# Gathering the expert rows in another order, and the index copy behind the sixteenth dot

## The chip, the cores and the metric

The kernel runs on one core of one Trainium2 chip. The metric is the device time of the whole kernel in microseconds (us): 2663.45, the median of 3 runs (2663.09 to 2665.34).

## The reference

Two transformer blocks follow each other on 256 tokens of 2048 channels, all in float32. The change touches only the last stage of the second block, a retrieval of single-neuron experts ("PEER"), whose core is this:

```python
def chunk(zc):                                   # 128 tokens
    ...                                          # key scores, top 16 of each half, top 16 of the sums
    u = jnp.take(peer_u, expert, axis=0)         # expert: 128 tokens x 8 heads x 16
    act = jax.nn.gelu(jnp.einsum('chkd,cd->chk', u, zc))
    v = jnp.take(peer_v, expert, axis=0)
    w = (gate * act.astype(jnp.float32)).astype(zc.dtype)
    return jnp.einsum('chk,chkd->cd', w, v).astype(zc.dtype)
```

peer_u and peer_v have 16384 rows of 2048 floats (8 KB each). For every token and head 16 rows of either table are read.

## The kernel before

The first half of the kernel (up to about 1266 us) is dense matrix products, and the change doesn't touch it. The expert stage works in 16 **rows**, one for each half of the tokens (hf) and head; a row is 128 tokens, one for each partition, and 16 experts for each token, k = 0 to 15. Both halves run as a hardware loop over pairs of rows (par = 0, 1), so there are two loops of four turns on VectorE (DVE), ScalarE and TensorE (PE), and GpSimd (POOL) runs one loop of seven turns with the last two rows behind it.

For each row r and each k two **gathers** are made, indirect DMAs of 1 MB which fetch 8 KB for each of the 128 tokens: **U k** from peer_u into one of four buffers ubuf, **V k** from peer_v into one of four buffers vbuf (slot s = k % 4). GpSimd issues them all, in the order in which its program has them (`gather`, L590 to L596; in the trace the issue stands at L595). Each gather first waits until its slot is free.

What is done with them:

- VectorE waits for U k and makes a **dot** with the normed token (L1493), a product of two 128x2048 tiles with a sum into column k of act. The end of the dot frees the slot of ubuf (u_free).
- After the sixteenth dot it makes asq (L1497), ain (L1499), er (L1502), agx (L1504) and wk (L1508), with a tanh on ScalarE in between. wk holds the 16 weights of the row. Then comes `choose` (L1410), the **sort**: some 28 small dependent steps, which pick the experts of row r + 2 and leave their numbers in expf.
- ScalarE turns a weight k into a diagonal matrix (L972), and TensorE multiplies it with V k into four banks of PSUM, eight instructions of 128x512 (L1870). Their end frees the slot of vbuf (v_free). So V k of a row can be used only once the wk of its row is there, after all 16 dots of that row.

The U gathers run one row ahead of the V gathers: while V of row r is fetched, so is U of row r + 1. Here is the order of GpSimd in a row: V 0, V 1, V 2, then V 3, U 0, V 4, U 1 and so on up to V 15, U 12, and last U 13, U 14, U 15 of row r + 1 with no V between (LAG = 3, L604 to L611).

The row numbers for the gathers are in idx, two sets of columns taken in turn (par). The set which V of row r - 1 used is written anew for U of row r + 1 by the **index copy** (L1487), which stands ahead of dot 12. It waits until TensorE has used V 15 of row r - 1 (L1486), because that gather reads the old set. U 0 of row r + 1 waits for the copy (idx_ready, in `gather_u`, L598).

Of the kernel before, what the change touches and what calls it, by code (L numbers as in the profile page):

```python
# [36 lines left out]
PEER_HEADS, KEYS, TOPK = 8, 128, 16  # L37
# [104 lines left out]
def build(nc, T, out):  # L142
# [3 lines left out]
    with ctx:  # L146
        def sb(name, shape, dt=f32):
            return ctx.enter_context(nc.sbuf_tensor(name, shape, dt))

        S = {n: ctx.enter_context(nc.semaphore(n)) for n in ONCE + LOOPED}  # L150
# [4 lines left out]
        v_landed = [ctx.enter_context(nc.semaphore(f"v_landed{s}")) for s in range(4)]  # L155
        v_free = [ctx.enter_context(nc.semaphore(f"v_free{s}")) for s in range(4)]
# [17 lines left out]
        def view(region, at, *dims):  # L174
            n = int(np.prod(dims))
            v = region[:, at:at + n]
            if len(dims) == 1:
                return v
            names = "abcd"[:len(dims)]
            return v.rearrange(f"p ({' '.join(names)}) -> p {' '.join(names)}", **dict(zip(names, dims)))  # L180
# [63 lines left out]
        vbuf = [view(EX, (4 + s) * D, D) for s in range(4)]  # L244
# [47 lines left out]
        expf = sb("expf", [P, TOPK])  # L292
        idx = sb("idx", [P, 2, TOPK], u32)
# [39 lines left out]
        peer_u, peer_v = T["peer_u_2"][0], T["peer_v_2"][0]  # L333
# [117 lines left out]
        def _(g):  # L451
# [15 lines left out]
            for s in range(2):  # L467
                v = dup[:, s, :].rearrange("p (a n) -> p a n", a=2)
# [11 lines left out]
            for at, reps, n, step, base in parts:  # L480
                v = dist[:, at:at + reps * n].rearrange("p (a n) -> p a n", a=reps)
# [5 lines left out]
            for s, base in enumerate((CMP_LEN - 1, CMP_LEN - 1 - P)):  # L487
                v = cmask[:, s * NCP:(s + 1) * NCP]
# [101 lines left out]
            def gather(table, buf, landed, free, r, par, k):  # L590
                s = k % 4

                g.wait_ge(free[s], r * 4 + (k // 4 + 1))
                g.nop(nofuse=True)
                g.indirect_dma_start(buf[s], None, table,  # L595
                                     bass.IndirectOffsetOnAxis(ap=idx[:, par, k:k + 1], axis=0)).then_inc(landed[s], 16)  # L596

            def gather_u(r, par, k):  # L598
                if k == 0:

                    g.wait_ge(S["idx_ready"], r + 1)
                gather(peer_u, ubuf, u_landed, u_free, r, par, k)

            LAG = 3  # L604

            def gather_row(r, par, last=False):
                for k in range(TOPK + LAG):
                    if k < TOPK:
                        gather(peer_v, vbuf, v_landed, v_free, r, par, k)
                    if k >= LAG and not last:  # L610
                        gather_u(r + 1, 1 - par, k - LAG)  # L611

            for k in range(TOPK):
                if k in (0, 2):
# [5 lines left out]
            with g.Fori(0, ROWS // 2 - 1) as i:  # L620
                for par in range(2):
                    gather_row(i * 2 + par, par)
            gather_row(ROWS - 2, 0)
            gather_row(ROWS - 1, 1, last=True)


# [356 lines left out]
        def _(v):  # L983
# [470 lines left out]
            for j in range(8):  # L1454
# [12 lines left out]
                if j >= 1:  # L1467
                    v.wait_ge(S["sc_evac"], 1 if j < 5 else 2)
                    for part in {1: (0,), 2: (1,), 3: (2,), 4: (3,), 5: (4,), 6: (5, 6), 7: (7,)}[j]:
                        r = part // 4  # L1470
# [6 lines left out]
            for hf in range(HALVES):  # L1477
                with v.Fori(0, PEER_HEADS // 2) as i:
                    for par in range(2):
                        r = i * 2 + (PEER_HEADS * hf + par)  # L1480

                        for k in range(TOPK):
                            s = k % 4
                            if k == TOPK - 4:

                                v.wait_ge(v_free[3], r * 4 + 1)  # L1486
                                v.tensor_copy(idx[:, 1 - par, :], expf[:]).then_inc(S["idx_ready"], 1)  # L1487
                                v.wait_ge(S["idx_ready"], r + 2)
                            v.wait_ge(u_landed[s], r * 64 + 16 * (k // 4 + 1))
                            if k >= 2:  # L1490

                                v.wait_ge(u_free[(k - 2) % 4], r * 4 + ((k - 2) // 4 + 2))
                            v.tensor_tensor_reduce(out=junk[k % 2], in0=ubuf[s], in1=znat[:, hf, :], scale=1.0, scalar=0.0,  # L1493
                                                   op0=ALU.mult, op1=ALU.add, accum_out=act[:, par, k:k + 1]).then_inc(u_free[s], 1)
                        v.wait_ge(u_free[3], r * 4 + 5)

                        v.tensor_tensor(asq[:], act[:, par, :], act[:, par, :], ALU.mult).then_inc(S["gel_step"], 1)  # L1497
                        v.wait_ge(S["gel_step"], r * 3 + 1)
                        v.scalar_tensor_tensor(ain[:, par, :], asq[:], 1.0 / GELU_C, act[:, par, :], op0=ALU.add, op1=ALU.mult)\  # L1499
                            .then_inc(S["inner_ready"], 1)  # L1500
                        v.wait_ge(S["ex_done"], r + 1)
                        v.reciprocal(er[:, par:par + 1], es[:, par:par + 1]).then_inc(S["gel_step"], 1)  # L1502
                        v.wait_ge(S["gel_step"], r * 3 + 2)
                        v.scalar_tensor_tensor(agx[:, par, :], act[:, par, :], er[:, par:par + 1], eg[:, par, :], op0=ALU.mult, op1=ALU.mult)\  # L1504
                            .then_inc(S["gel_step"], 1)
                        v.wait_ge(S["gel_step"], r * 3 + 3)
                        v.wait_ge(S["gel_done"], r + 1)
                        v.scalar_tensor_tensor(wk[:, par, :], ath[:, par, :], 1.0, agx[:, par, :], op0=ALU.add, op1=ALU.mult)\  # L1508
                            .then_inc(S["w_ready"], 1)

                        v.wait_ge(S["sc_evac"], PEER_HEADS)
                        choose(r + 2, par, r * CHOOSE + 2 * CHOOSE)
# [384 lines left out]
```

## Time and profile before

| | |
|---|---|
| median of 3 runs | 2663.45 us |
| the profiled execution | 2671.37 us |
| its span, first to last instruction | 2669.6 us |
| busy: PE / DVE / POOL / ACT | 84% / 57% / 29% / 26% |
| L1870, products of the expert stage | 959.5 us, 2048 instructions |
| L1493, dots | 582.4 us, 256 instructions of 2291 ns |
| L595, gathers issued for V and U | 331.7 us and 295.9 us, 256 each |
| gathers, issue to landing | V 12.5 us, U 13.1 us (median) |
| moved by the gathers' queue | 539.07 MB in all |

The page cuts the span into 40 slices of 66.7 us; the expert stage is the last 20 of them. "Idle before" and the name behind the arrow in a row of the timeline tell how long the engine had nothing to do ahead of the instruction, and who released it. A row of the timeline begins with the start in us from the span's start and the duration in us.

### The profile page before, as it was taken

The page shows a single profiled execution, that of the slowest core. Times are in us where ns is not written, and L with a number is a line of the kernel's source. Part 1 is how long each engine was busy: PE and PEld are TensorE (multiplying, and loading weights), DVE is VectorE, ACT ScalarE, POOL GpSimd, SP SyncE. Part 2 cuts the span into 40 slices and gives each one's busy share as a digit, 9 for nine tenths or more (in the row PEclk, how much of TensorE's full clock was granted, in tenths as well). Part 3 has the DMA queues.
Part 4 walks back from the last instruction along what each step waited for, and adds up shares of the span by engine and source line. Part 5 has one row for each costly group of instructions (what it writes and reads, how often), then busy time and mean ns, then how long its engine had stood idle before and what let it go on. Part 6 is the DMA issues. An engine that isn't in the chain of part 4 may idle for free.

```text
span 2669.6 us, 33108 instructions
## 1 busy us (share of the span) xinstructions
PE 2230.4 (84%) x12212; PEld 1633.3 (61%) x12212; DVE 1528.6 (57%) x2181; ACT 694.6 (26%) x1151; POOL 772.3 (29%) x658
## 2 busy tenths in 40 slices
PE   7999999999999999899567668777687766877668
PEld 7999999999999999899522223222232322322223
DVE  4455555455646686656665555665556555566552
ACT  5344554444434435444100000000000000000001
POOL 3000000000002433120354444544445444444441
PEclk9999999999999999999788999998999889989899
DMA  9534444455675444565699999999999999999996
GB/s 260 184 127 142 141 143 140 157 163 169 213 228 177 142 158 158 154 193 158 234 394 396 400 423 393 400 402 390 416 401 400 389 386 423 402 387 403 388 423 248
DMA packets 280704, 754.61 MB, mean 283 GB/s; under 512 B 11968, under 2 KB 213152, under 8 KB 213792
## 3 DMA queue, kind: packets, MB, share of 16 engines
q0 software_dynamic: 74432, 539.07, 49.7%
q1 hardware_dynamic: 205936, 214.23, 25.3%
q8 instruction: 56, 0.92, 0.1%
q14 instruction: 40, 0.33, 0.0%
q10 hardware_dynamic: 240, 0.07, 0.0%
HBM read 751.22 MB, written 2.10 MB: 282 GB/s over the span
## 4 chain that ended last, share of the span: by engine, by line
PE 59%; DMA 25%; issue 7%; DVE 7%; POOL 1%; ACT 1%; DVEq 0%; POOLq 0%; ACTq 0%; SPq 0%
PE PS L1552 39%; DMA EX<-in_peer_v,idx 22%; PE PS L1870 14%; DVE EX L1493 2%; DMA RAW<-in_peer_u,idx 2%; PE PS L1687 1%; DVE WL L993 1%; POOL EX L595 1%; PE PS L1607 1%; PE PS L1665 1%; DVE XL L1003 0%; PE PS L1675 0%; PE PS L1787 0%; POOL RAW L595 0%; PE PS L1689 0%
## 5 line engine op out<-in xcount | busy, mean ns | idle before, releaser
L1870 PE MATMUL PS<-EX,RK 128*128 128x512 f32 x2048 | 959.5, 620 | 396.5 <-ACT RK L972 207.8
L1870 PEld LDWEIGHTS PS<-EX,RK 128*128 128x128 f32 x2048 | 390.9, 197 | 964.5 <-issue 902.2
L1552 PE MATMUL PS<-XH,WH 128*128 128x256 f32 x3024 | 839.1, 286 | 11.7 <-DVE WL L993 8.0
L1493 DVE CUSTOM_DVE_ANT_0 EX<-RAW,RZ 128x2048 f32<-128x2048 f32 x256 | 582.4, 2291 | 449.7 <-DMA RAW<-in_peer_u,idx 422.1
L1552 PE MATMUL PS<-XH,WL 128*128 128x256 f32 x3024 | 832.7, 284 | 0.0
L1552 PE MATMUL PS<-XL,WH 128*128 128x256 f32 x3024 | 761.9, 284 | 5.0 <-DVE XL L1003 3.1
L993 DVE TENSOR_TENSOR WL<-RAW,WH 128x1024 fp32r<-128x1024 f32 x380 | 479.7, 1274 | 413.5 <-ACT WH L643 410.9
L1552 PEld LDWEIGHTS PS<-XH,WH 128*128 128x128 f32 x3024 | 582.0, 192 | 15.7 <-issue 9.7
L1552 PEld LDWEIGHTS PS<-XH,WL 128*128 128x128 f32 x3024 | 582.2, 193 | 0.0
L643 ACT ACTIVATE WH<-RAW 128x1024 fp32r<-128x1024 f32 x380 | 400.2, 1059 | 566.1 <-PE PS L1552 564.5
L1552 PEld LDWEIGHTS PS<-XL,WH 128*128 128x128 f32 x3024 | 539.9, 193 | 5.9 <-DVE XL L1003 3.5
L595 POOL DMA_INDIRECT EX<-in_peer_v,idx x256 | 331.7, 1296 | 464.9 <-PE PS L1870 408.9
L595 POOL DMA_INDIRECT RAW<-in_peer_u,idx x256 | 295.9, 1156 | 362.4 <-DVE act L1493 211.8
L972 ACT ACTIVATE RK<-identh,wk 128x128 f32<-128x128 f32 x256 | 97.5, 399 | 759.7 <-PE PS L1870 752.8
L508 POOL TENSOR_SCALAR_AFFINE_SELECT RG<-RG 128x1024 f32<-128x1024 f32 x1 | 1.1, 1088 | 512.8 <-ACT RG L776 512.8
L966 ACT ACTIVATE ath<-ain 128x16 f32<-128x16 f32 x16 | 3.5, 216 | 483.1 <-DVE ain L1499 483.1
L514 POOL TENSOR_TENSOR RK<-RZ 128x512 f32 x16 | 17.1, 1067 | 215.5 <-DVE RZ L1259 148.8
L530 POOL MEMSET RK<- 128x1024 f32 x1 | 1.0, 954 | 181.3 <-PE PS L1759 181.3
L753 ACT ACTIVATE RG<-RG,nmx 128x256 f32<-128x256 f32 (+2 forms) x96 | 37.7, 394 | 45.7 <-DVE nmx L1146 45.7
L1487 DVE CAST idx<-expf 128x16 uint32<-128x16 f32 x16 | 3.0, 185 | 60.1 <-PE PS L1870 60.1
L567 POOL TENSOR_TENSOR RZ<-RZ 128x540 f32<-128x540 f32 (+3 forms) x10 | 15.1, 1507 | 55.3 <-DVE RZ L1291 54.8
L515 POOL TENSOR_TENSOR RK<-RK 128x512 f32<-128x512 f32 x16 | 26.9, 1681 | 1.3
(316 smaller groups left out, 1139.1 us busy)
## 6 DMA issues: line engine op xcount, KB each, us to landing
RAW<-in_w_in SPq DMA_DIRECT2D x110, 1024.0 KB, 5.1
RAW<-in_w_out SPq DMA_DIRECT2D x32, 1024.0 KB, 5.4
RAW<-in_w_ple_gate SPq DMA_DIRECT2D x16, 1024.0 KB, 5.4
RAW<-in_peer_wq SPq DMA_DIRECT2D x16, 1024.0 KB, 5.4
RAW<-in_w_up_a SPq DMA_DIRECT2D x8, 1024.0 KB, 5.4
RAW<-in_w_up_b SPq DMA_DIRECT2D x8, 1024.0 KB, 5.3
RAW<-in_peer_u,idx POOLq DMA_INDIRECT x256, 13.1
EX<-in_peer_v,idx POOLq DMA_INDIRECT x256, 12.5
```

The lines of the kernel that those rows point to most:

```text
L515: step(g.tensor_tensor(acc[:, 0], acc[:, 0], sqt[:, 0], ALU.add))
L595: g.indirect_dma_start(buf[s], None, table, bass.IndirectOffsetOnAxis(ap=idx[:, par, k:k + 1], axis=0)).then_inc(landed[s], 16)
L643: a.activation(WH[:, q], raw[:, slot, at:at + QUARTER_KT, :], ACT.Copy).then_inc(S["wh_ready"], 1)
L753: ins = a.activation(eT[:, at:at + size], sT[:, at:at + size], ACT.Exp, bias=nmx[:, n:n + 1], accum_out=sums[:, n:n + 1])
L972: a.activation(diag[:, s, :], identh[:], ACT.Copy, scale=wk[:, par, k:k + 1]).then_inc(diag_ready[s], 1)
L993: v.tensor_tensor(WL[:, q], raw[:, slot, at:at + QUARTER_KT, :], WH[:, q].bitcast(f32), ALU.subtract).then_inc(S["wl_ready"], 1)
L1493: v.tensor_tensor_reduce(out=junk[k % 2], in0=ubuf[s], in1=znat[:, hf, :], scale=1.0, scalar=0.0, op0=ALU.mult, op1=ALU.add, accum_out=act ...
L1552: ins = mm(o[:, t, :], w[:, q, k, c], x[:, n, :], start=(begins and k == t == m == 0), stop=(ends and k == QUARTER_KT - 1 and m == len(pai ...
L1607: ins = mm(bank(2 + s)[0:SPANS, 0:P], blocks, w1bd[:, s, l, :], start=(l == 0), stop=(l == CMP_LEN - 1))
L1665: mm(pS[:, 0:512], q1, kpad[:, par, :, bass.ds(i, 1), :].rearrange("p t g n -> p (t g) n"), start=True, stop=True)
L1687: mm(pO[:, at:at + size], vcur[:, n, cols], pts[:, src:src + size], start=(par == 0 and n == 0), stop=False, skip_group_check=True)
L1870: ins = mm(bank(4 * hf + c), diag[:, s, :], vbuf[s][:, 512 * c:512 * (c + 1)], start=False, stop=True, skip_group_check=True)
```

## The change

GpSimd's order becomes V 0, V 1, V 2, V 3, then U 0 to U 3 of the next row together, and from there V k, U k in turn up to V 15, U 15. The index copy, with its two waits, moves from ahead of dot 12 to behind ain, that is behind the sixteenth dot and ahead of er. No instruction is added or left out.

```diff
-            LAG = 3
+            HEAD = 4
 
             def gather_row(r, par, last=False):
-                for k in range(TOPK + LAG):
-                    if k < TOPK:
-                        gather(peer_v, vbuf, v_landed, v_free, r, par, k)
-                    if k >= LAG and not last:
-                        gather_u(r + 1, 1 - par, k - LAG)
+                for k in range(TOPK):
+                    gather(peer_v, vbuf, v_landed, v_free, r, par, k)
+                    if k >= HEAD - 1 and not last:
+                        for ahead in range(HEAD) if k == HEAD - 1 else (k,):
+                            gather_u(r + 1, 1 - par, ahead)
...
                         for k in range(TOPK):
                             s = k % 4
-                            if k == TOPK - 4:
-
-                                v.wait_ge(v_free[3], r * 4 + 1)
-                                v.tensor_copy(idx[:, 1 - par, :], expf[:]).then_inc(S["idx_ready"], 1)
-                                v.wait_ge(S["idx_ready"], r + 2)
                             v.wait_ge(u_landed[s], r * 64 + 16 * (k // 4 + 1))
...
                         v.scalar_tensor_tensor(ain[:, par, :], asq[:], 1.0 / GELU_C, act[:, par, :], op0=ALU.add, op1=ALU.mult)\
                             .then_inc(S["inner_ready"], 1)
+                        v.wait_ge(v_free[3], r * 4 + 1)
+                        v.tensor_copy(idx[:, 1 - par, :], expf[:]).then_inc(S["idx_ready"], 1)
+                        v.wait_ge(S["idx_ready"], r + 2)
                         v.wait_ge(S["ex_done"], r + 1)
```

## Rows read from the trace of the kernel before

**Rows 1.** The page: GB/s moved in 40 slices, and the chain's shares by engine.

```profile
GB/s 260 184 127 142 141 143 140 157 163 169 213 228 177 142 158 158 154 193 158 234 394 396 400 423 393 400 402 390 416 401 400 389 386 423 402 387 403 388 423 248
...
PE 59%; DMA 25%; issue 7%; DVE 7%; POOL 1%; ACT 1%; DVEq 0%; POOLq 0%; ACTq 0%; SPq 0%
```

**Rows 2.** Windows (us, busy of each engine, PEclk, DMA share, GB/s) of a row's turn.

```profile
1930.00:1938.00 8.00, 5.61 (x7) 2.52 (x8) 6.52 (x28) 1.49 (x5) 0.00 (x0) 0.50 1.02 424
1938.00:1942.00 4.00, 4.00 (x10) 1.72 (x10) 3.06 (x13) 0.40 (x1) 1.87 (x2) 0.99 0.30 88
```

**Rows 3.** Timeline of GpSimd at the same turn: U 13, V 2, U 0, V 4.

```profile
1908.23 0.93 POOL L595 DMA_INDIRECT RAW<-in_peer_u,idx  x1 [3.71 <-DVE act L1493]
...
1921.91 3.03 POOL L595 DMA_INDIRECT EX<-in_peer_v,idx  x1 [0.30 <-issue]
...
1927.46 1.91 POOL L595 DMA_INDIRECT RAW<-in_peer_u,idx  x1 [0.30 <-issue]
1939.73 0.94 POOL L595 DMA_INDIRECT EX<-in_peer_v,idx  x1 [10.36 <-PE PS L1870]
```

**Rows 4.** Timeline of VectorE at it: dot 15, asq, dots 0 and 1 of the next row.

```profile
1928.48 2.29 DVE L1493 CUSTOM_DVE_ANT_0 EX<-RAW,RZ 128x2048 f32<-128x2048 f32 x1
...
1930.81 0.17 DVE L1497 TENSOR_TENSOR asq<-act 128x16 f32<-128x16 f32 x1
...
1944.88 2.29 DVE L1493 CUSTOM_DVE_ANT_0 EX<-RAW,RZ 128x2048 f32<-128x2048 f32 x1 [0.50 <-DVE expf L1450]
...
1948.01 2.29 DVE L1493 CUSTOM_DVE_ANT_0 EX<-RAW,RZ 128x2048 f32<-128x2048 f32 x1 [0.83 <-DMA RAW<-in_peer_u,idx]
```

**Rows 5.** Timeline of TensorE: V 15, the next row's V 0 on, V 11 and V 15.

```profile
1917.70 3.67 PE L1870 MATMUL PS<-EX,RK 128*128 128x512 f32 x8 [1.30 <-DMA EX<-in_peer_v,idx]
1932.39 27.10 PE L1870 MATMUL PS<-EX,RK 128*128 128x512 f32 x56 [11.02 <-ACT RK L972]
...
1980.95 3.67 PE L1870 MATMUL PS<-EX,RK 128*128 128x512 f32 x8 [1.14 <-DMA EX<-in_peer_v,idx]
...
2000.82 3.67 PE L1870 MATMUL PS<-EX,RK 128*128 128x512 f32 x8 [1.29 <-DMA EX<-in_peer_v,idx]
```

**Rows 6.** The page's group of the index copy: busy, mean ns, idle before it.

```profile
L1487 DVE CAST idx<-expf 128x16 uint32<-128x16 f32 x16 | 3.0, 185 | 60.1 <-PE PS L1870 60.1
```

**Rows 7.** Waits from 1345.30 to 2601.83: us in total, times, longest us.

```profile
DVE EX L1493 <- issue: 19.4, 3, 6.7
...
DVE EX L1493 <- DVE idx L1487: 3.5, 15, 0.2
```

**Rows 8.** asq in all rows: number, min/median/max ns, first and last start.

```profile
L1497 DVE TENSOR_TENSOR asq<-act x16: 174/174/175, 1345.3 to 2601.8; 128x16 f32<-128x16 f32 x16
```

**Rows 9.** Timeline of VectorE: asq of rows 1, 9, 10, 12, 13, 14.

```profile
1429.40 0.17 DVE L1497 TENSOR_TENSOR asq<-act 128x16 f32<-128x16 f32 x1
...
2097.86 0.17 DVE L1497 TENSOR_TENSOR asq<-act 128x16 f32<-128x16 f32 x1
...
2183.21 0.17 DVE L1497 TENSOR_TENSOR asq<-act 128x16 f32<-128x16 f32 x1
...
2351.49 0.17 DVE L1497 TENSOR_TENSOR asq<-act 128x16 f32<-128x16 f32 x1
...
2434.46 0.17 DVE L1497 TENSOR_TENSOR asq<-act 128x16 f32<-128x16 f32 x1
...
2518.78 0.17 DVE L1497 TENSOR_TENSOR asq<-act 128x16 f32<-128x16 f32 x1
```

**Rows 10.** Timeline behind asq of row 9: dot 0 and the issue of U 4.

```profile
2118.07 2.29 DVE L1493 CUSTOM_DVE_ANT_0 EX<-RAW,RZ 128x2048 f32<-128x2048 f32 x1 [6.54 <-issue]
...
2121.14 2.24 POOL L595 DMA_INDIRECT RAW<-in_peer_u,idx  x1 [3.09 <-DVE act L1493]
```

**Rows 11.** DMA from 2097.86 to 2117.86, an instruction queue: packets, MB, share.

```profile
q14 instruction: 2, 0.02, 0.3%
```

**Rows 12.** Timeline of TensorE: the 16 V of the last row.

```profile
2603.41 57.00 PE L1870 MATMUL PS<-EX,RK 128*128 128x512 f32 x128 [11.01 <-ACT RK L972]
```

## The prediction

> **What bounds the kernel now.** I read the page's slices and chain first. In the last 20 slices the core moves 384 to 423 GB/s, where the dense half moves 127 to 260 for the most part [rows 1]. TensorE's 59% of the chain and the DMAs' 25% say little by themselves, since in the expert stage each V lands, is used, and frees a slot [rows 1]. So the question is whether the transfers ever run dry. In the middle of a row they don't: V 11 and V 15 are used 19.87 us apart, which is four pairs of gathers, 2.484 us a gather and 4.97 a pair [rows 5], and 424 GB/s is the rate of a full queue [rows 2]. A row has 32 gathers, so no row can take less than 32 x 2.484 = 79.5 us. An undisturbed one takes 2434.46 - 2351.49 = 82.97 us from asq to asq [rows 9]. The 3.5 us between are seen in the windows: 88 GB/s from 1938 to 1942, a loss of 4 x (1 - 88/424) = 3.2 us [rows 2].
>
> Next, the timeline tells why. Behind U 0 (issued at 1927.46) GpSimd issues nothing until V 4 at 1939.73, because V 4 needs the slot of V 0 [rows 3]. V 0 can't be used before wk, and TensorE starts it 1.58 us behind asq, after 11.02 us without work [rows 4, 5]. At the granted clock of 0.50 (the 1.2 GHz level; the window in which TensorE starts after that idle time) V 0 needs until 1938.95, if I take the 0.78 us that GpSimd takes to follow the end of a dot (2118.07 + 2.29 to 2121.14) for the end of a V too [rows 2, 3, 10]. That is 6.56 us in place of the 3.67 of other V [rows 5]. The gathers issued until then run out at about 1938. asq in turn is late, since the copy waits for V 15 (60.1 us in all 16 rows) and the last four dots come behind it [rows 6].
>
> **The new order at a row's turn.** I count from the use of V 15 of row r - 1 as time 0. The queue then lands U 15 at 2.48, V 0 to V 3 of row r at 4.97 to 12.4, U 0 to U 3 of row r + 1 at 14.9 to 22.4, and V 4 at 24.8. A gather that finds the queue empty needs, from the end of its issue until it can be used, 4.86 us: V 4's issue ends at 1940.67 and the dot on U 1, the second gather behind the gap, starts at 1948.01, 7.34 less 2.48 [rows 3, 4]. Now each against its turn:
> - V 3 has its slot at 3.67 + 0.78, its issue takes 0.94 [rows 3, 5], so it could be used at 10.3, ahead of 12.4. V 0 to V 2 have their slots before. Hidden.
> - U 15 arrives with nothing before it in the dots' way: asq is at 2.48 + 2.33 = 4.8 [rows 4]. The copy's wait for V 15 is over at 3.67, so the wait that cost up to 4 us per row ends. The copy costs 0.185 us plus 0.2 for the wait on its own semaphore, 0.4 in all, and it is now ahead of wk and of the sort [rows 6, 7]. What stands behind this wait on VectorE is er, agx, wk, the sort and the next dots; on GpSimd, U 0 and all gathers after it.
> - U 0 is released at 5.4 and usable at 11.2 (its turn: 14.9). U 1 to U 3 follow 1.24 us apart. V 4 needs V 0's end: TensorE starts at 4.8 + 1.58 + 0.4 = 6.8 after only 3.1 us of idle time, V 4 would be usable at 17, or at 20 if V 0 takes 6.56, and its turn is 24.8. So the gap of before closes.
> - **U 4** is late next. It needs dot 0, and dot 0 stands behind the sort: 1944.88 - 1930.81 = 14.07 us after asq, plus 0.4 for the copy [rows 4]. From the start of dot 0 to the end of U 4's issue there is one row that shows just this, dots back to back: 2118.07 to 2121.14 + 2.24 = 2123.38, 5.31 us [rows 10]. So U 4 is usable at 4.8 + 14.5 + 5.3 + 4.9 = 29.4, and its turn is 27.3. V 5 and all others stand behind it. A gap of 2.1 us replaces that of 3.5.
>
> After that, issues among back-to-back dots end once per dot, 2.2 us apart, and the queue takes 2.48, so it doesn't run dry again. From U 4 to U 15 are 22 turns, 54.65 us, and the new row takes 14.5 + 5.3 + 4.9 + 54.65 + 2.33 = **81.6 us**, 1.35 less than 82.97.
>
> The 2.24 us of U 4's issue against 0.94 elsewhere are part of this price. An issue that begins while a dot runs ends 0.88 us behind that dot's end: V 2, issued at 1921.91 during a dot, took 3.03 [rows 3, 10]. The Trainium skill, SBUF — State Buffer, "Who interferes with whom", says that VectorE and GpSimd share a port pair that the first to start holds for its whole instruction, and that a VectorE instruction with two SBUF inputs holds up those of GpSimd that read SBUF. The trace agrees: 3.03 against 0.94. Without such a hold, U 4's issue would end 1.3 us sooner, and the 14 full turns would gain 18 us more.
>
> **Where VectorE pauses.** Dot 0 is behind its row's asq by 14.07 us, but by 20.21 after asq of row 9 (2097.86 to 2118.07), and the idle time before it is put down to nothing but issue [rows 9, 10]. There are 3 such waits, 19.4 us [rows 7], all where the second half's loop turns back, and meanwhile an instruction queue moves packets [rows 11]. Now this is on slack: its rows take 85.35 and 84.32 us (rows 9 and 13), the third lies between, 1.9 over a row without it [rows 9]. In the new order U 4 waits for dot 0, so the pause of 6.1 is paid in full: 81.6 + 6.1 = 87.7, which is 2.9 us slower than now, or 4.8 if the 1.9 are something else that stays. I take the middle, 3.8 each. The loop bodies keep their instructions, so I expect the pauses to stay. The Trainium skill, Runtime: NRT & Kernel Launch, "Instruction fetch mechanics", says that a taken branch to a target outside the fetched window must first fetch it by DMA. The trace agrees with the place and the queue.
>
> **The sum** (us):
> - first turn: now 1429.40 - 1345.3 = 84.1, then 81.6: -2.5 [rows 8, 9];
> - 11 turns without pause: 11 x -1.35 = -14.9;
> - 3 turns with pause: 3 x 3.8 = +11.4;
> - the last row: its 57.00 us on TensorE have no U beside them and are bound by TensorE [rows 12]. 3.1 us of idle time instead of 11 leaves V 0 at 3.67, -2.9 (0 if the clock falls all the same); the copy +0.4. Together -2.5.
>
> That is -8.5. The profiled execution took 2671.37 with a span of 2669.6, 7.9 over the median (0.3%); I carry the difference over to the median: 2663.45 - 8.5 = **2655.0**. From the bounds: pauses at 2.9 or 4.8 give -11.2 or -5.5; a cold V 0 at the end gives -5.6; 0.3 us more or less per turn for an unqueued gather gives 4.5 either way. The likeliest case's own range is 2648 to 2662.
>
> **The rivals.** About 0.2% (5.3 us) is what can be told from no change.
> - *The pauses go* (10%). If the moved steps shift where the loop's code falls, these three turns also gain 1.35 each, and the 3 x 1.9 that they cost now if these are the pause's: -2.5 - 14 x 1.35 - 2.5 = -23.9, and -29.6 with them: 2634 to 2639.5. For it: the first half's three turns with the same body have no such pause [rows 7]. Against: the count of instructions doesn't change.
> - *The hold is less* (5%): U 4's issue isn't held up, -8.5 - 14 x 1.3: 2637. Against it are 3.03 and 2.24.
> - *The gap only moves* (13%). If U 4 is usable 0.5 us later than I count, 15 turns cost 7.5: 2662.5, no difference. For it: the price of an unqueued gather rests on one place.
> - *Slower* (12%): the sort pays. In the new order five issues (U 0 to U 3, V 4) fall into wk and the first half of the sort, where now there is none before 1939.73 [rows 3]. If the shared port makes one step of VectorE wait for one issue of 0.94 us in each of 15 turns, that is +14.1, and 2669. It decides from 8.5 / 15 = 0.57 us per turn on. Against it: the issue at 1939.73 falls into the sort now, and the 14.07 us already contain it.
> - The likeliest case has 60%: of these 42 over 0.2% faster, 17 within, 1 slower.
>
> Faster: 42 + 10 + 5 = 57%. Within 0.2%: 17 + 11 of the third rival = 28%. Slower: 12 + 2 + 1 = 15%. The range of 2636 to 2669 leaves out part of the first two rivals and half of the slower one.
>
> **What the profile would show.** Right: V 4 is no longer released by TensorE after 10 us of idle time; U 4 has the long wait on a dot instead, and its issue takes over 2 us. The copy has no idle time before it. Rows of 81.6 us and three of 87.7. TensorE sits idle for about 3 us before V 0, with the clock at 2.4 GHz. The low window in GB/s is about 2 us long and follows V 4. Wrong: a wait before V 3 or U 0 in which the rate falls; asq to dot 0 over 14.8 us; a second low window behind U 4; rows 9, 11, 13 no longer than their neighbours.

## The result

The changed kernel takes 2676.27 us (median of 6 runs, 2674.31 to 2681.12), where the kernel before takes 2663.22. The ratio is 1.0054, 95% interval 1.0041 to 1.0067: slower by half a per cent, some 13 to 14 us, where 8.5 us less were forecast. In the next section it is measured once more, at 2681.89 us and 1.0073 (1.0048 to 1.0099). The span of the profiled execution is 2673.5 us.

The rates and the chain of the page after. Beside [rows 1], TensorE has 8 points less of the chain and VectorE 4 more, and the slices of the expert stage are as full as before.

```profile
GB/s 261 183 126 133 149 144 141 149 166 173 208 222 183 137 167 158 154 193 158 237 397 399 398 415 402 404 400 403 421 404 405 360 407 418 363 403 361 423 400 264
...
PE 51%; DMA 26%; DVE 11%; issue 8%; POOL 3%; ACT 1%; DVEq 0%; POOLq 0%; SPq 0%; ACTq 0%
```

A row's turn in the timeline of GpSimd after (the order is V 4, U 4, V 5, U 5), to be read beside [rows 3]:

```profile
2016.02 0.93 POOL L595 DMA_INDIRECT EX<-in_peer_v,idx  x1 [0.37 <-issue]
2026.83 2.25 POOL L595 DMA_INDIRECT RAW<-in_peer_u,idx  x1 [9.88 <-DVE act L1488]
2029.38 1.90 POOL L595 DMA_INDIRECT EX<-in_peer_v,idx  x1 [0.30 <-issue]
2031.59 1.90 POOL L595 DMA_INDIRECT RAW<-in_peer_u,idx  x1 [0.30 <-issue]
```

V 4 no longer waits for TensorE (0.37 instead of 10.36 us). The long wait is now U 4's, for the end of dot 0, and three issues in a row take about 2 us each. The same turn on VectorE, with asq, the index copy, and dots 0, 4, 5 and 6 (beside [rows 4]; the dot stands at L1488 now):

```profile
2009.64 0.17 DVE L1492 TENSOR_TENSOR asq<-act 128x16 f32<-128x16 f32 x1
...
2009.94 0.17 DVE L1497 CAST idx<-expf 128x16 uint32<-128x16 f32 x1
...
2023.76 2.29 DVE L1488 CUSTOM_DVE_ANT_0 EX<-RAW,RZ 128x2048 f32<-128x2048 f32 x1 [0.22 <-DVE expf L1450]
...
2034.15 2.29 DVE L1488 CUSTOM_DVE_ANT_0 EX<-RAW,RZ 128x2048 f32<-128x2048 f32 x1 [1.46 <-DMA RAW<-in_peer_u,idx]
...
2040.95 2.29 DVE L1488 CUSTOM_DVE_ANT_0 EX<-RAW,RZ 128x2048 f32<-128x2048 f32 x1 [4.50 <-DMA RAW<-in_peer_u,idx]
...
2046.02 2.33 DVE L1488 CUSTOM_DVE_ANT_0 EX<-RAW,RZ 128x2048 f32<-128x2048 f32 x1 [2.77 <-DMA RAW<-in_peer_u,idx]
```

The copy no longer waits. Dot 0 is 14.12 us behind asq, dot 4 10.39 behind dot 0. Then comes what the prediction had named as a sign of being wrong, a second slow stretch behind U 4: from dot 4 to dot 5 are 6.80 us, where a pair of gathers takes 4.97. The windows of the turn show it too (us, busy of each engine, PEclk, DMA share, GB/s), beside [rows 2]:

```profile
2016.00:2024.00 8.00, 8.00 (x20) 3.55 (x19) 6.10 (x22) 0.80 (x2) 0.93 (x1) 1.00 1.02 425
2024.00:2030.00 6.00, 1.55 (x4) 0.38 (x2) 6.00 (x5) 0.40 (x1) 2.87 (x2) 1.00 0.85 318
2030.00:2034.00 4.00, 3.71 (x5) 1.50 (x6) 2.70 (x4) 0.00 (x0) 3.39 (x3) 0.62 0.87 334
2034.00:2036.00 2.00, 1.69 (x4) 0.52 (x2) 1.85 (x1) 0.27 (x1) 1.70 (x2) 0.91 1.02 389
2036.00:2038.00 2.00, 0.00 (x0) 0.00 (x0) 0.45 (x2) 0.13 (x1) 1.70 (x2) 0.95 1.00 373
2038.00:2040.00 2.00, 1.41 (x2) 0.84 (x3) 0.00 (x0) 0.00 (x0) 1.43 (x2) 0.50 1.00 410
```

The deep hole of before (88 GB/s for 4 us) is gone. In its place the rate is below 425 for 16 us. Against 425 that is a loss of 1.5 + 0.9 + 0.2 + 0.2 + 0.1 = 2.9 us (each window's length times one minus its rate over 425). It was 3.2 before.

Behind rows 9, 11 and 13 VectorE pauses as it did (3 waits put down to issue, 17.7 us in all). Here is dot 0 behind row 9, whose asq is at 2092.93, and the asq of row 10, 88.57 later [rows 9, 10]:

```profile
2112.87 2.29 DVE L1488 CUSTOM_DVE_ANT_0 EX<-RAW,RZ 128x2048 f32<-128x2048 f32 x1 [5.83 <-issue]
...
2181.50 0.17 DVE L1492 TENSOR_TENSOR asq<-act 128x16 f32<-128x16 f32 x1
```

### The profile page after: what moved, and what is told of

Its sections match the earlier page's. It is cut to its first block, busy times and chain, and to the rows that moved or that the text cites. A ratio compares the mean times of both kernels' runs of the same rounds, so it can differ in the third digit from the quotient of the medians.

```text
span 2673.5 us, 33116 instructions
## 1 busy us (share of the span) xinstructions
PE 2260.4 (85%) x12212; PEld 1639.7 (61%) x12212; DVE 1529.4 (57%) x2181; ACT 694.8 (26%) x1151; POOL 771.3 (29%) x658
## 4 chain that ended last, share of the span: by engine, by line
PE 51%; DMA 26%; DVE 11%; issue 8%; POOL 3%; ACT 1%; DVEq 0%; POOLq 0%; SPq 0%; ACTq 0%
PE PS L1550 39%; DMA EX<-in_peer_v,idx 13%; DMA RAW<-in_peer_u,idx 13%; PE PS L1868 6%; DVE EX L1488 2%; POOL RAW L595 2%; POOL EX L595 1%; PE PS L1685 1%; DVE WL L993 1%; DVE RK L1426 1%; PE PS L1605 1%; DVE RK L1446 1%; DVE RK L1448 1%; DVE pick L1449 1%; PE PS L1663 1%
## 5 line engine op out<-in xcount | busy, mean ns | idle before, releaser
L1868 PE MATMUL PS<-EX,RK 128*128 128x512 f32 x2048 | 987.2, 633 | 370.9 <-DMA EX<-in_peer_v,idx 286.2
L1488 DVE CUSTOM_DVE_ANT_0 EX<-RAW,RZ 128x2048 f32<-128x2048 f32 x256 | 583.5, 2293 | 511.4 <-DMA RAW<-in_peer_u,idx 488.9
L595 POOL DMA_INDIRECT EX<-in_peer_v,idx x256 | 298.9, 1167 | 498.1 <-PE PS L1868 453.3
L595 POOL DMA_INDIRECT RAW<-in_peer_u,idx x256 | 327.7, 1280 | 332.4 <-DVE act L1488 167.5
```

Source lines behind the costliest of these rows:

```text
L595: g.indirect_dma_start(buf[s], None, table, bass.IndirectOffsetOnAxis(ap=idx[:, par, k:k + 1], axis=0)).then_inc(landed[s], 16)
L1868: ins = mm(bank(4 * hf + c), diag[:, s, :], vbuf[s][:, 512 * c:512 * (c + 1)], start=False, stop=True, skip_group_check=True)
```

## The experiments

All rows of a kernel can be taken from the starts of asq and of the dots in its timeline. The table has the mean lengths, in us; "ordinary" are the turns without pause, the first one left out. The last column is the time from the first asq to the last.

```
profiled execution        first   ordinary (n)   with pause (3)   all 15
before                    84.10   83.46 (11)     84.81            1256.5
before, second profile    83.62   82.97 (11)     84.58            1250.1
after                     83.78   82.85 (11)     88.87            1261.7
after, second profile     82.84   83.26 (11)     88.40            1263.9
copy only                 83.19   82.03 (11)     83.52            1236.0
before, loops written out 83.75   82.69 (14)     -                1241.4
after, loops written out  83.91   82.72 (14)     -                1241.9
V 4-7 ahead of U 4        82.04   80.23 (11)     82.80            1212.9
sort in parts             82.29   80.79 (14)     -                1213.4
order only                91.22   91.08 (11)     94.00            1375.1
U 4 later, written out    88.04   87.39 (14)     -                1311.5
V 4-7, written out        80.44   80.52 (14)     -                1207.7
V 4-7, parts, written out 84.60   80.59 (14)     -                1212.8
```

**Both kernels again.** No edit.

> The kernel before, once more, for a second profile of it. The first one took 2671.4 us where its median is 2663.2, so something in that execution cost 8 us. If that is chance in the transfers, the rows here differ from the first profile in single rows and the three pauses stay. If the pauses themselves vary, asq to dot 0 behind rows 9, 11 and 13 differs from 20 us. The median should be 2663 either way.

> The changed kernel, once more, beside the others: 2676 in the median. Theory (dot 0 of the next row holds back U 4, and with it all transfers): undisturbed rows again near 82.5 us, those behind a pause near 88.8, U 4 issued 3.1 us after dot 0 in each row.

Before: 2664.46 us, ratio 1.0006 (0.9992 to 1.0019). After: 2681.89, ratio 1.0073. The second profile of the kernel before is 6.4 us shorter in its rows than the first, by single rows between 82.0 and 85.1 that come out otherwise, while the three pauses are there again. So an ordinary row isn't a fixed figure, and the 82.97 on which the forecast counted is one of the short ones in the first profile, whose mean is 83.46. The two profiles of after have ordinary rows of 82.85 and 83.26 and rows with pause of 88.87 and 88.40; near 82.5 and 88.8 were expected.

**Only the index copy is moved.** GpSimd keeps the old order (LAG = 3).

```diff
-                            if k == TOPK - 4:
-                                v.wait_ge(v_free[3], r * 4 + 1)
-                                v.tensor_copy(idx[:, 1 - par, :], expf[:]).then_inc(S["idx_ready"], 1)
-                                v.wait_ge(S["idx_ready"], r + 2)
...
+                        v.wait_ge(v_free[3], r * 4 + 1)
+                        v.tensor_copy(idx[:, 1 - par, :], expf[:]).then_inc(S["idx_ready"], 1)
+                        v.wait_ge(S["idx_ready"], r + 2)
```

> Only the index copy is moved, the gathers keep the old order. Theory: asq no longer waits for V 15, but for U 15, which the old order lands 9.9 us behind V 15; asq then comes 12.3 us behind V 15 instead of 13.1, and the wait of V 4 for V 0 stays. Rows 0.4 to 0.8 us shorter, 2652 to 2658, and the pauses cost no more than before. Rival (the copy ahead of wk and the sort is what costs): slower than before, by 0.3 us a row or more, 2668 and up.

2650.74 us, ratio 0.9953 (0.9936 to 0.9970): faster, and the rival falls. asq now follows the use of V 15 by 1920.08 - 1907.92 = 12.2 us instead of 13.1 [rows 4, 5]. Ordinary rows of 82.03 are 1.2 us under the mean of both profiles of before (83.2), more than the 0.4 to 0.8 expected; where the rest comes from I haven't traced.

**Only the order is changed.** The copy stays ahead of dot 12.

> Only the order of the gathers is changed, the copy stays ahead of dot 12. Theory: the last four dots wait for V 15, which now lands just ahead of U 15; asq comes 13.1 us behind V 15, dot 0 at 27, and U 4 is usable at 37.5 where its turn is 27.3, a gap of 10 us in each row: 89 to 91 us a row, 95 to 97 behind a pause, some 2780 us. Rival (the order is harmless and the copy's place is what costs): within 10 us of before.

2796.08 us, ratio 1.0503 (1.0474 to 1.0532), 5% slower. The page's group of the copy, beside [rows 6], says where: its wait for V 15 has grown from 60.1 to 283.8 us.

```profile
L1487 DVE CAST idx<-expf 128x16 uint32<-128x16 f32 x16 | 2.8, 175 | 283.8 <-PE PS L1870 283.8
```

V 15 now lands next to U 15, and dot 12, which could have started with U 12, waits for it. An ordinary row takes 90.4 to 92.4 us, some 91 on average, at the upper end of what was expected. The pauses of rows 9, 11 and 13 are shorter there: dot 0 comes 16.7 to 16.9 us behind asq and not 20, and these rows take 93.6 to 94.7 us, where 95 to 97 were expected. Why they are shorter isn't shown. So the two parts of the change belong together: the new order needs the later copy. The later copy doesn't need the new order, and is worth 11 us without it.

**No turn of the loop on VectorE.** Its two loops of the expert stage written out, in the changed kernel and in the one before.

```diff
-                with v.Fori(0, PEER_HEADS // 2) as i:
+                for i in range(PEER_HEADS // 2):
```

> The changed kernel with VectorE's two loops of the expert stage written out, so that nothing turns back there. Theory (the three pauses of 5.7 us come from the loop's turn, and are paid in full because U 4 waits for dot 0): all rows near 83, no wait of over 5 us put down to issue; 3 x 5.6 = 17 us faster than the changed kernel, 2660 to 2665. Rival (the longer rows 9, 11, 13 come from the transfers, not from the loop): 2677 to 2682 as now.

> The kernel before with the same loops written out. Theory: there dot 0 is on slack, and only the 1.4 to 1.8 us by which rows 9, 11, 13 are longer can go: 2657 to 2663, at most 5 us faster. If it gains 15 us or more, the pauses were paid before as well, and they don't explain what the change lost.

After: 2658.20 us, ratio 0.9983 (0.9970 to 0.9996), 18 to 24 us faster than the changed kernel with its loops. Before: 2652.73, ratio 0.9963 (0.9949 to 0.9977), 10.7 us faster. In neither trace is a wait of over 3 us put down to issue, and all dots 0 come 13.7 to 14.3 us behind asq. The pauses do come from the loop's turn, and the changed kernel pays more for them. The rows then come to the same sum, 1241.9 and 1241.4 us. The medians of ten executions are still 5.5 us apart, the changed kernel being the slower. The two profiles are 3.1 us apart, of which 2.6 lie ahead of the first asq, where the change touches nothing; the difference of the medians stays open. That the kernel before gains 10.7 and not 5 at most is a miss: the three rows with pause account for 3 x (84.7 - 82.7) = 6, the rest is in ordinary rows (82.69 against 82.97 and 83.46), and I haven't traced it.

The queue of instructions tells the loop that pauses from the one that doesn't. In both profiles of the kernel before, this queue (q14) moves nothing from row 2 to row 6, though the first half's loop turns back behind rows 3 and 5. It moves 4 packets in each of rows 9, 11 and 13, and 1 or 2 in each of rows 10, 12 and 14.

**V 4 to V 7 ahead of U 4.** In the changed kernel V 4 stands ahead of U 4 already; here V 5, V 6 and V 7 do too, so that more is in the queue while U 4 waits.

```diff
-            HEAD = 4
+            HEAD, LAG = 4, 3
...
-                for k in range(TOPK):
-                    gather(peer_v, vbuf, v_landed, v_free, r, par, k)
-                    if k >= HEAD - 1 and not last:
-                        for ahead in range(HEAD) if k == HEAD - 1 else (k,):
-                            gather_u(r + 1, 1 - par, ahead)
+                for k in range(TOPK + LAG):
+                    if k < TOPK:
+                        gather(peer_v, vbuf, v_landed, v_free, r, par, k)
+                    if k == HEAD - 1 and not last:
+                        for ahead in range(HEAD):
+                            gather_u(r + 1, 1 - par, ahead)
+                    elif k >= HEAD + LAG and not last:
+                        gather_u(r + 1, 1 - par, k - LAG)
```

> The changed kernel, but after V 0-3 and U 0-3 GpSimd issues V 4 to V 7 ahead of U 4, then V 8, U 5 and so on; the row ends with U 13, U 14, U 15. Theory (all is held behind U 4, which waits for a dot behind the sort): with three V more in the queue U 4's turn comes at 42 us behind V 15, and it is usable at 37, so no gap is left: 79.6 to 80.5 us a row, 2600 to 2620, and the pauses are hidden but for about 1 us. Rival (the loss of the changed kernel lies in the burst of V 0-3 and U 0-3 or in the copy's place): both stay here, so no better than 2660.

2625.57 us, ratio 0.9863 (0.9842 to 0.9884): 38 us faster than before and 51 faster than the changed kernel, 6 us over the range that I expected. The burst and the copy's place are innocent, since both are in it. In the first half five of the eight rows are 79.50 to 79.58 us, what 32 gathers cost; one is 79.74, and the first and the seventh are 82.04 and 80.87. Two starts of asq, and the window between them:

```profile
1583.48 0.17 DVE L1495 TENSOR_TENSOR asq<-act 128x16 f32<-128x16 f32 x1
1662.99 0.17 DVE L1495 TENSOR_TENSOR asq<-act 128x16 f32<-128x16 f32 x1
```

```profile
1583.48:1662.99 79.51, 60.07 (x128) 24.64 (x128) 47.49 (x77) 6.60 (x19) 39.56 (x32) 0.93 1.01 418
```

In the second half they take 80.8 to 81.8, and 81.4 to 83.8 behind a pause. So a pause still costs 0.6 to 3.0 us over 80.8, where I expected about 1.

**The sort in four parts**, behind dots 4, 5, 7 and 9, for the next row instead of the one after it; the gathers in the order of the change. The sort of row 1, which the kernel before and the changed one make ahead of the expert stage, moves into row 0 with it.

```diff
...
                                                    op0=ALU.mult, op1=ALU.add, accum_out=act[:, par, k:k + 1]).then_inc(u_free[s], 1)
+                            if k == 4:
+                                v.wait_ge(S["sc_evac"], PEER_HEADS)
+                            if k in (4, 5, 7, 9):
+                                choose(r + 1, 1 - par, r * CHOOSE + CHOOSE, ((4, 5, 7, 9).index(k),))
...
-                        v.wait_ge(S["sc_evac"], PEER_HEADS)
-                        choose(r + 2, par, r * CHOOSE + 2 * CHOOSE)
```

> The changed kernel, its gathers' order kept, but the sort doesn't stand between the rows: the sort for row r + 1 is done in four parts behind dots 4, 5, 7 and 9 of row r. Theory: dots 0 to 3 start as their U land (14.9 to 22.4 us behind V 15), U 4 is usable well before its turn, no gap and no pause is left on the path: 79.6 to 80.5 us a row, 2600 to 2620. If the second low window (behind U 4) comes from issues held up by back-to-back dots, it goes as well. Rival (the gap has another cause, such as the burst): rows over 82 us.

2628.78 us, ratio 0.9875 (0.9855 to 0.9895). In the second half dot 0 starts 10.1 us behind asq, when its U lands, no pause shows, and the last five rows take 79.47 to 79.55 us each. The window over one of them has the full rate throughout:

```profile
2241.00:2321.00 80.00, 59.84 (x128) 23.84 (x128) 48.06 (x78) 6.60 (x19) 40.70 (x33) 0.98 1.01 422
```

In the first half three rows (1, 3 and 5) take 83.0 to 83.4 us; in these dot 0 comes 11.6 to 12.0 us behind asq. I can't explain it, and so the whole is 9 us over what I expected. This version takes away what U 4 waits behind, and the one before it takes away what waits behind U 4; they are 47 and 51 us faster than the changed kernel, which had lost 13. That U 4, held back by a dot behind the sort, empties the queue is shown by this.

**U 4 later still.** It waits for dot 3; the loops are written out. The question is the step from U 4 to U 5.

```diff
                 if k == 0:
                     g.wait_ge(S["idx_ready"], r + 1)
+                if k == 4:
+                    g.wait_ge(u_free[3], r * 4 + 2)
```

> The changed kernel with VectorE's loops written out (no pauses), and U 4 made to wait for dot 3 instead of dot 0, so the queue is empty for 6.6 us longer in each row and the issues of V 5, U 5 and V 6 no longer stand between back-to-back dots. What is asked is why U 5 and U 6 are used 6.1 and 5.6 us apart there where 4.97 is the pace. If the dots that hold up the issues are the cause, those steps fall to 5.0 to 5.2 us and issues take 0.94. If a queue that starts from empty is slow in its first gathers whatever the issues do, the steps stay at 5.5 to 6.2. In both cases a row is some 5 to 7 us longer, 15 times: 2735 to 2765 us.

2730.54 us, ratio 1.0255 (1.0232 to 1.0277); 2735 to 2765 were expected. A turn on GpSimd and on VectorE (U 4, V 5, U 5, then the dots on U 4, U 5 and U 6):

```profile
1985.72 0.94 POOL L595 DMA_INDIRECT RAW<-in_peer_u,idx  x1 [16.38 <-DVE act L1490]
1986.96 0.93 POOL L595 DMA_INDIRECT EX<-in_peer_v,idx  x1 [0.30 <-issue]
1988.20 0.94 POOL L595 DMA_INDIRECT RAW<-in_peer_u,idx  x1 [0.31 <-issue]
```

```profile
1991.27 2.29 DVE L1490 CUSTOM_DVE_ANT_0 EX<-RAW,RZ 128x2048 f32<-128x2048 f32 x1 [6.34 <-DMA RAW<-in_peer_u,idx]
1997.55 2.29 DVE L1490 CUSTOM_DVE_ANT_0 EX<-RAW,RZ 128x2048 f32<-128x2048 f32 x1 [3.98 <-DMA RAW<-in_peer_u,idx]
2002.51 2.29 DVE L1490 CUSTOM_DVE_ANT_0 EX<-RAW,RZ 128x2048 f32<-128x2048 f32 x1 [2.66 <-DMA RAW<-in_peer_u,idx]
```

Issues take 0.94 again, and still U 5 comes 6.28 us behind U 4. Means over all rows, U 4 to U 5 and U 5 to U 6: 5.72 and 4.98 here, 5.91 and 5.52 in the same kernel without the wait, 6.1 to 6.2 and 5.5 to 5.7 in the two profiles of the changed kernel. So neither expectation holds alone. The first pair behind an empty queue is slow even when no issue is held up, by some 0.8 us over the steady 4.97. The second pair's excess of 0.5 is gone here. That it goes because the issues aren't held up is the likely reading, but not shown alone: the queue is also empty for longer here. Why the first pair is slow stays open.

**Towards a faster version.** V 4 to V 7 ahead of U 4, with the loops written out; and the same with the sort in parts.

> V 4 to V 7 ahead of U 4, and VectorE's loops written out. Theory: the rows of the first half were at 79.5 to 79.7 us already, those of the second at 80.8, or 81.4 to 83.8 behind a pause; without the turn of the loop all are at 79.5 to 80.5, some 12 us less than with it: 2608 to 2618. If the second half stays at 80.8 a row, that excess is not from the loop's turn.

> V 4 to V 7 ahead of U 4, the sort in four parts behind dots 4, 5, 7 and 9, and the loops written out. If the transfers are the bound once neither the slots nor the sort hold them back, this can't be better than 32 x 2.484 = 79.5 us a row, so it equals the version without the parts: 2605 to 2618. If it is clearly faster, rows were still held by something other than the queue.

2620.90 us, ratio 0.9849 (0.9829 to 0.9868), and 2627.65, ratio 0.9871 (0.9853 to 0.9888). The first is the fastest version of the study, 1.5% under the kernel before, and 3 us over the range that I expected. Its rows take 79.8 to 81.2 us: those of the second half are no longer than those of the first now, but those of the first aren't at 79.5 either. Written out, the loops gain 5 us here and not 12. With the parts on top I expected the same time, and it is 7 us longer. In the profiles 5 us of that lie in the rows, 4 of them in the first (84.60 against 80.44), and 6 ahead of the expert stage; I haven't traced it.

## Why the prediction was wrong

**What bounds the kernel** was right: the transfers, wherever the queue runs dry. The floor of 79.5 us a row was reached by single rows in two experiments. A small misreading of [rows 1]: the last 20 slices run from 386 to 423 GB/s, with 248 in the very last, and not from 384.

**The new order at a turn** was right down to the wait. V 0 to V 4 are hidden, the copy's wait is gone, U 4 is late behind dot 0. Dot 0 behind asq took 14.25 us (14.5 forecast), from dot 0 to the use of U 4 10.0 (10.2), the end of the row 2.34 (2.33). The hold of an issue by a dot came as priced: 2.25 us for U 4. (Held issues end 0.80 to 0.82 us behind the end of the dot, by the durations of the rows; the prediction's 0.88 is a slip without effect.) The Trainium skill's rule on the shared port (SBUF — State Buffer, "Who interferes with whom") and the trace agree once more: 1.90, 1.90 and 2.25 us among back-to-back dots, 0.94 where the dots are over.

One sign came out wrong without costing anything at these turns: V 0 was to find the clock at 2.4 GHz. TensorE does start it after less than 3 us of idle time, but the granted clock over the 4.5 us from 1.5 us behind asq is 0.50 to 0.70 in 11 of the 15 turns of the first profile and in 13 of the second, and 1.00 in the rest. Two of these windows, behind rows 7 and 8:

```profile
1928.94:1933.44 4.50, 4.20 (x5) 1.83 (x6) 3.47 (x17) 1.05 (x4) 3.58 (x4) 0.50 1.02 424
2011.14:2015.64 4.50, 4.09 (x10) 1.94 (x11) 3.38 (x17) 1.51 (x5) 3.58 (x4) 1.00 1.01 422
```

The rate stays full in both, since V 4 has slack enough either way, as the prediction had it.

**The step that failed** is "so it doesn't run dry again", with the term made of it, 22 turns in 54.65 us. It measured 56.31 and 56.69. I had compared issues that end every 2.2 us with a queue that takes 2.48, and let the queue run at its full pace from the first gather. It doesn't: the first pair behind the gap takes some 0.8 us longer even when its issues are early, and the second some 0.5 longer in the changed kernel, where they are held up. Together with single disturbed steps, of which each profile has some, that is 1.85 us a row. The undisturbed row of before already has a restart in its 82.97, and my row of after had hardly any.

The trace of before had this price, in rows that I didn't read. I took it from one turn, 7.34 us from the end of V 4's issue to the dot on U 1 [rows 3, 4]. That is the lowest of all 15 turns: over the ordinary ones the mean is 8.26 us, and 8.00 in the second profile. Here is the turn behind row 10, with 2201.36 - 2193.11 = 8.25:

```profile
2192.17 0.94 POOL L595 DMA_INDIRECT EX<-in_peer_v,idx  x1 [10.40 <-PE PS L1870]
```

```profile
2201.36 2.29 DVE L1493 CUSTOM_DVE_ANT_0 EX<-RAW,RZ 128x2048 f32<-128x2048 f32 x1 [1.98 <-DMA RAW<-in_peer_u,idx]
```

With the mean of 8.26 in place of the one turn the new row would have come to some 82.5 us, and the gain of an ordinary turn to some 0.4. That is an estimate from these rows. It puts the whole price ahead of U 4, which is usable 4.6 to 4.8 us behind its issue on average, while the excess comes with the pairs behind it.

**The reference row** was also chosen too neatly, though this works the other way: 82.97 is a short row in a profile whose ordinary rows average 83.46 (second profile: 82.97). The forecast of -1.35 a turn became 83.06 - 83.21 = -0.15, the means of two profiles each. Over 11 turns that is -1.7 instead of -14.9, and it is most of the error.

**The pauses** were right in their mechanism, they are paid in full: 3 x 3.8 = +11.4 forecast, and 88.64 - 84.70 = 3.9 each, +11.8, measured. That the size fits so well is partly luck. Written out, the kernel before loses the 1.9 us by which its rows with pause were longer, so they were the pause's own, and by the prediction's own terms 2.9 would have been the choice, with a row of 87.7. It came to 88.64 because the row beneath it is 1.5 us longer than forecast, while the pause adds 5.6 and not 6.1. Writing out the loops shows that the pauses are the loop's turn, and that the change pays them: with them gone the two kernels' rows have the same sum. The Trainium skill (Runtime: NRT & Kernel Launch, "Instruction fetch mechanics") says that a taken branch to a target outside the fetched window has to wait for its fetch. The trace agrees: the loop that pauses moves 4 instruction packets in each row with a pause, and the one that doesn't moves none from row 2 to row 6.

**The first turn and the last row** gave -0.5 instead of -2.5 and -0.3 instead of -2.5. In the first turn the same slow restart took most of the gain. In the last row TensorE starts V 0 after 2.84 us of idle time as forecast, and its 16 V take 55.20 us from 2609.12 in the first profile (57.00 before). But in the second profile it is 58.2, and there the granted clock is 0.50 (the 1.2 GHz level) in the first 4.2 us of that row, after the same 2.84 us of idle time. The prediction had named this case (0 instead of -2.9 if the clock falls all the same).

```profile
2609.12 11.42 PE L1868 MATMUL PS<-EX,RK 128*128 128x512 f32 x26 [2.84 <-ACT RK L972]
...
2659.44 4.88 PE L1868 MATMUL PS<-EX,RK 128*128 128x512 f32 x11
```

The sum by measured terms is -0.5 - 1.7 + 11.8 - 0.3 = +9.3, which is the mean difference of the two pairs of profiles: spans of 3.9 and 14.8 us more. The timed medians are 13 and 17 to 20 us apart; what lies between that and 9.3 stays open, with two profiles of each and executions of one kernel that spread over 7 to 15 us.

**The rivals.** The pauses didn't go by themselves, and U 4's issue is held up. "The gap only moves" is what happened in ordinary rows, by a mechanism near the one named: U 4 is usable when I said, but what follows it is slower. It got 13% and 0.5 us a turn; measured are 1.5 us a turn over the 81.6, so its 2662.5 was too low as well. The slower rival was the wrong one: the sort doesn't pay for the five issues beside it. Dot 0 is 14.25 us behind asq, of which 14.05 are the old value and the rest the copy.

## What to carry to other kernels

When a gap in a full queue is moved rather than filled, count the restart as part of its price. Here a queue that was empty gave its first transfers more slowly than its steady pace, and a schedule that adds up steady turns behind the gap promises a gain that isn't there. Take such a price from all turns of the trace: the one turn used here was the lowest of 15. To fill a gap, look for what can be issued ahead of the late one (here three more V gathers, 51 us off the changed kernel), before making a wait shorter. And where one engine issues everything in a fixed order, every later issue stands behind the latest one. A slack that covered a pause of another engine is gone the moment the next issue waits for that engine.

## What the runs showed of the hardware

- A 1 MB gather that finds the queue empty can be used 4.4 to 5.1 us after its issue ends (U 4 in the changed kernel and in the version that holds it back longer, apart from one turn of 6.7; the means are 4.6 to 4.8). The steady pace is 2.484 us a gather (418 to 424 GB/s over whole rows and stretches of it). The pair after it comes 5.7 to 6.2 us later on average instead of 4.97, with issues unhindered or not.
- The turn of VectorE's loop of about 80 steps and 32 dots costs 0.2 to 0.5 us in the first half and 5.4 to 6.3 us each time in the second, whose body is the same (2.7 to 3.0 where only the order was changed). Written out, both halves run without it. The half that pauses moves instruction packets in each row, the other none from its third row to its seventh.
- The eleven ordinary rows of one trace, with the same instructions, differ by up to 2.7 us (82.68 to 85.33 before). Two profiles of one kernel differ by 6 us in the sum of 15 rows. A forecast of 1.35 us a row needs the mean of all rows on its other side, not one row.
